# A hybrid decoder step on one core: two more weight slots, key turns and weights moved ahead of state traffic, first merge's products beside its gate

## The reference

```python
h = rms_norm(x, lw['norm_w'])
proj = jnp.einsum('bsd,de->bse', h, lw['w_in']) + lw['b_in']
# A: gated DeltaNet (conv, chunks of the delta rule, per-head state), gate dn_z
# B: RG-LRU (conv, gates, scan), gate lru_g
# C: forgetting attention: fq = rms_norm(fq), fk = rms_norm(fk), fv, decay logf, gate fg
# M: cross-attention into 256 memory tokens, gate mg
mk, mv = jnp.split(jnp.einsum('bmd,de->bme', rms_norm(mem, w), w_mem_kv), 2)   # prompt's memory keys, values
branches = jnp.stack([out_a, out_b, out_c, out_m], axis=2)
up = jnp.einsum('bsnw,nwd->bsnd', branches, lw['w_branch'])
gates = jax.nn.sigmoid(mgate.reshape(bn, s, N_BRANCH, D_MODEL))
y = x + jnp.einsum('bsd,de->bse', jnp.sum(gates * up, axis=2), lw['w_out'])
```

## Time and profile before

| | us |
|---|---|
| median of 3 runs (1779.48 to 1781.74) | 1780.54 |
| the profiled execution | 1779.63 |
| its span, first to last instruction | 1777.9 |
| PE busy in it (95%) | 1683.3 |
| PE loading weights (90%, beside the matmuls) | 1609.0 |
| DVE busy (44%) | 787.0 |
| ACT busy (30%) | 533.3 |
| POOL busy (29%) | 512.5 |

### The profile page before, as it was taken

One profiled execution on the slowest core, in us unless ns is written; L12 is line 12 of the kernel. 1 busy time (PEld: TensorE's weight loads), 2 busy tenths in 40 slices (PEclk: granted clock), 3 DMA queues, 4 the chain that ended last, 5 costly groups with the idle time before them and its releaser, 6 DMA issues. The chain is left out here.

```text
span 1777.9 us, 26816 instructions
## 1 busy us (share of the span) xinstructions
PE 1683.3 (95%) x11027; PEld 1609.0 (90%) x11027; DVE 787.0 (44%) x1199; ACT 533.3 (30%) x895; POOL 512.5 (29%) x388
## 2 busy tenths in 40 slices
PE   5999998999999998899999999999999989999999
PEld 5899998999999998899889898999989988899976
DVE  5485742333333334550365511145657540744711
ACT  6223333222222222132234323221145212554300
POOL 1343325333344314511344431212211121012310
PEclk9999999999999999899999999999999999999999
DMA  4211144222222115423255341234310332433531
GB/s 135 49 39 48 48 131 134 66 66 66 54 66 66 48 48 160 142 72 92 88 165 154 104 146 66 90 96 154 84 47 14 108 96 66 142 98 114 159 94 54
DMA packets 189367, 163.21 MB, mean 92 GB/s; under 512 B 18381, under 2 KB 157056, under 8 KB 188727
## 3 DMA queue, kind: packets, MB, share of 16 engines
q1 hardware_dynamic: 189246, 161.51, 31.0%
HBM read 131.38 MB, written 30.22 MB: 91 GB/s over the span
## 5 line engine op out<-in xcount | busy, mean ns | idle before, releaser
L258 POOL TENSOR_TENSOR wL<-w_raw,wH 128x1024 fp32r<-128x1024 f32 (+1 forms) x114 | 247.4, 2170 | 887.6 <-ACT wH L251 887.6
L282 PE MATMUL ps<-hH,wH 128*128 128x344 f32 x1920 | 449.3, 343 | 27.0 <-POOL wL L258 11.0
L282 PE MATMUL ps<-hL,wH 128*128 128x344 f32 x1920 | 412.2, 323 | 0.0
L282 PE MATMUL ps<-hH,wL 128*128 128x344 f32 x1920 | 409.8, 322 | 0.0
L282 PEld LDWEIGHTS ps<-hH,wH 128*128 128x128 f32 x1920 | 315.1, 192 | 40.5 <-issue 23.6
L282 PEld LDWEIGHTS ps<-hL,wH 128*128 128x128 f32 x1920 | 328.3, 191 | 0.0
L282 PEld LDWEIGHTS ps<-hH,wL 128*128 128x128 f32 x1920 | 325.3, 190 | 0.0
L251 ACT ACTIVATE wH<-w_raw 128x1024 fp32r<-128x1024 f32 (+1 forms) x120 | 112.7, 939 | 124.4 <-PE ps L282 99.3
L2743 POOL TENSOR_SCALAR fa_logits<-fox_c_bc,token_scalars 128x128 f32<-128x128 f32 (+7 forms) x32 | 58.2, 1820 | 67.5 <-PE ps L2768 50.1
L2886 DVE SCALAR_TENSOR_TENSOR fa_logits<-ps,fox_rq,fa_logits 128x512 f32<-128x512 f32 (+3 forms) x48 | 28.2, 612 | 106.5 <-POOL fa_logits L2744 59.6
L1730 ACT ACTIVATE d_m<-ps 128x512 f32<-128x512 f32 x48 | 28.6, 595 | 142.3 <-PE ps L1906 142.3
(11 more groups left out here) (558 smaller groups left out, 2815.2 us busy)
## 6 DMA issues: line engine op xcount, KB each, us to landing
w_raw<-in_w_in SPq DMA_DIRECT2D x80, 512.0 KB, 5.3
m_th<-gate_spill SPq DMA_DIRECT2D x28, 516.0 KB, 4.3
gate_spill<-d_gate SPq DMA_DIRECT2D x18, 516.0 KB, 3.0
fa_kv<-in_cache_fox_k SPq DMA_DIRECT2D x32, 256.0 KB, 3.1
fa_kv<-in_cache_fox_v SPq DMA_DIRECT2D x32, 256.0 KB, 3.1
w_raw<-in_w_branch SPq DMA_DIRECT2D x32, 256.0 KB, 2.9
gate_spill<-fa_gate SPq DMA_DIRECT2D x10, 516.0 KB
x_rows<-in_x_prompt SPq DMA_DIRECT2D x8, 512.0 KB, 6.5
```

Of the source, the lines that this page charges most:

```text
L258: pool.tensor_tensor(self.wL[:, t % 2, 0:nk], self.raw[:, t % 2, 0:nk], self.wH[:, t % 2, 0:nk].bitcast(F32), ALU.subtract).then_inc(self. ...
L282: last = pe.matmul(self.ps[:, b + g, 0:cols], w[:, t % 2, k], x[:, k, g * cols:(g + 1) * cols], start=(k == 0 and n == 0), stop=(k == nk - ...
```

## The change

Four edits that do not touch what is computed.

1. *Memory tiles.* Tiles 2, 3, 6 and 7 of the 8 memory tiles get raw slots of their own (2 and 3) in y_x, the memory rows' buffer, which is free when the 8 transposes are done (`raw_free`, mem_tr). wH and wL keep two slots. SP asks for the first two memory tiles ahead of the first two stores of the dn_z gate, and for tiles 2 and 3 ahead of the third. POOL no longer makes the low part of memory tile 1; DVE now makes those of tiles 1 to 7 (before: 2 to 7).
2. *fk.* The load of the fourth fk tile stands between the two halves of the decode state loads, and that of the first fv tile ahead of the wait for the query row. `POOL_AT` puts one state before the low part of fk tile 2 instead of three, three before that of fk tile 3 instead of six, and six before that of fv tile 0 instead of eight.
3. *fv.* ACT copies out the first five turns before it calls `before(act)`, which now stands ahead of the first tile's own copy.
4. *fg and the first merge.* DVE multiplies gate and branch right behind each gate part, and ACT rounds three of the four products inside the fg stage.

The tiles d_state, d_dT and d_w of the delta rule lie elsewhere in the on-chip buffer, so that they don't overlap y_x.

```diff
     def loads(self, sp, upto):
...
-            if t >= 2:
-                sp.wait_ge(self.w_lo, t - 1)
-            sp.dma_start(self.raw[:, t % 2, 0:nk], src).then_inc(self.w_loaded[t % 2], 16)
+            q, n, last = self.raw_use(t)
+            if t in self.raw_free:
+                sp.wait_ge(*self.raw_free[t])
+            if last is not None:
+                sp.wait_ge(self.w_lo, last + 1)
+            sp.dma_start(self.raw_at(t)[:, 0:nk], src).then_inc(self.w_loaded[q], 16)
...
+    def raw_slot(self, t):
+        return self.raw_of[t][0] if t in self.raw_of else t % 2
+
+    def raw_at(self, t):
+        return self.raw_of[t][1] if t in self.raw_of else self.raw[:, t % 2]
+
+    def raw_use(self, t):
+
+        q = self.raw_slot(t)
+        users = [u for u in range(t) if self.raw_slot(u) == q]
+        return q, len(users), users[-1] if users else None
...
@@ gate_branch
+                K.loads(sp, t0 + 4 + 2)
                 if spill is not None:
                     put(0)
                     put(1)
                 if side:
                     side.sync_last(sp)
-                K.loads(sp, t0 + 4 + 2)
                 if spill is not None:
+                    K.loads(sp, t0 + 4 + 4)
                     put(2)
-                    K.loads(sp, t0 + 4 + 3)
+                    K.loads(sp, t0 + 4 + 5)
                     put(3)
...
-                K.split_lo(pool, t0 + 4 + (2 if next_by_dve else 1))
+                K.split_lo(pool, t0 + 4 + 1)
...
                     act.activation(TH[:], G[:, slot(j)], ACT.Tanh).then_inc(th, 1)
+                    if then and j >= 1:
+                        then.act_hi(act, j - 1)
...
                     dve.scalar_tensor_tensor(g, TH[:], 1.0, g, ALU.add, ALU.mult).then_inc(silu, 1)
+                    if then:
+                        dve.wait_ge(silu, j + 1)
+                        then.dve_product(dve, j)
...
@@ Merge
-            for j in range(H):
+            for j in range(H - 1 if self.begun else 0, H):
                 self.br.act_hi(act, j)
...
-            if j < H:
+            if j < H and not self.begun:
                 self.br.dve_product(dve, j)
...
@@ UnitsAndMemory
+        for x, q in ((2, 2), (3, 3), (6, 2), (7, 3)):
+            K.raw_of[t_kv + x] = (q, self.X[:, q - 2].rearrange("p (k c) -> p k c", k=KD))
+            if x < 4:
+                K.raw_free[t_kv + x] = (self.Y["tr"], KD)
...
@@ DeltaDecode
-    POOL_AT = ((0, 1, 2), (3, 4, 5), (6, 7), ())
+    POOL_AT = ((0,), (1, 2), (3, 4, 5), (6, 7))
...
@@ project_tiles
-                    side.sync_first(sp)
+                    side.sync_first(sp, 0)
+                    K.loads(sp, t0 + 4)
+                    side.sync_first(sp, 1)
                     for j in range(2):
-                        K.loads(sp, t0 + 4 + j)
+                        K.loads(sp, t0 + 5 + j)
                         side.sync_part(sp, j)
...
-                    if j == 0 and fresh is None:
+                    if j == 0 and turned_first:
+                        act.wait_ge(*ready)
+                    elif j == 0 and fresh is None:
                         before(act)
...
                     for turn in of(j):
                         turns.act(act, turn)
+                    if j == 0 and turned_first:
+                        before(act)
                     act.wait_ge(K.tile_done, t + 1)
```

More of the change, by code:

```diff
@@ L152, in __init__ @@
         self.dn_convs = self.dn_space.enter_context(nc.sbuf_tensor("dn_conv_states", [P, 12, 24], F32))
-        self.w_loaded = [sem("w_loaded0"), sem("w_loaded1")]
+        self.w_loaded = [sem(f"w_loaded{q}") for q in range(4)]
         self.w_hi, self.w_lo = sem("w_hi"), sem("w_lo")
@@ L159, in __init__ @@
         self.at_load = self.at_hi = self.at_lo = 0
+        self.raw_of, self.raw_free = {}, {}
         self.v_sem, self.v_n = sem("vector_step"), [0]
@@ L247, in split_hi @@
             nk = self.tiles[t][1]
-            act.wait_ge(self.w_loaded[t % 2], 16 * (t // 2 + 1))
+            q, n, _ = self.raw_use(t)
+            act.wait_ge(self.w_loaded[q], 16 * (n + 1))
             if t >= 2:
                 act.wait_ge(self.tile_done, t - 1)
-            act.activation(self.wH[:, t % 2, 0:nk], self.raw[:, t % 2, 0:nk], ACT.Identity).then_inc(self.w_hi, 1)
+            act.activation(self.wH[:, t % 2, 0:nk], self.raw_at(t)[:, 0:nk], ACT.Identity).then_inc(self.w_hi, 1)
             self.at_hi = t + 1
@@ L905, in gate_branch @@
 def gate_branch(K, t0, name, G, tag, side=None, spill=None, fetch=None, fresh=False,
-                next_by_dve=False):
+                next_by_dve=False, then=None):
     nc = K.nc
@@ L1041, in __init__ @@
     def __init__(self, K, sb, t0, n, br, here, first=False, prepared=False, nxt=None, fetch=None,
-                 late=None):
-        self.late = late
+                 late=None, begun=False):
+        self.late, self.begun = late, begun
         self.K, self.t0, self.n, self.br, self.here = K, t0, n, br, here
@@ L1477, with __init__ @@
 class UnitsAndMemory(UnitFactors):
-    def __init__(self, K, kept, c, tail):
+    def __init__(self, K, kept, c, tail, t_kv):
         super().__init__(K, kept, c)
@@ L1572, in delta_rule @@
         two = lambda n_: sb(n_, [P, 2, H, P])
-        X, Y, ST, DT, W, M1, U, STG, O, SQ = (one(n_) for n_ in (
-            "_x", "_y", "_state", "_dT", "_w", "_m1", "_u", "_st_decayed", "_o", "_osq"))
+        X, Y, M1, U, STG, O, SQ = (one(n_) for n_ in ("_x", "_y", "_m1", "_u", "_st_decayed", "_o", "_osq"))
         NU, QKT, QG, VB, KBG, KD_ = (two(n_) for n_ in ("_nu", "_qkT", "_qgT", "_vb", "_kbg", "_kdec"))
+        ST, DT, W = (one(n_) for n_ in ("_state", "_dT", "_w"))
         RN, GC = units.RN, units.GC
@@ L2050, in load_rows, with sync_first @@
                      src.broadcast_to([P, n * H * P])).then_inc(sem, 16)
-    def sync_first(self, sp):
-        for b in range(NB):
+    def sync_first(self, sp, half):
+        for b in range(NB // 2 * half, NB // 2 * (half + 1)):
             if b % (NB // 2) == 0:
@@ L2343, in project_tiles @@
                   preload=True, side=None, late=None, ready=None, first=None, settle=None,
-                  fresh=None, early=(), by_dve=False):
+                  fresh=None, early=(), by_dve=False, turned_first=False):
     nc = K.nc
@@ L3176, in build @@
                 project_tiles(K, at["fv"], 4, BROW["fv"], VX, "fv", turns=turns,
-                              rows=(k_rows, sizes, K.knw, after), late=decode, ready=K.emptied(at["fv"] - 1),
+                              rows=(k_rows, sizes, K.knw, after), late=decode, ready=K.emptied(at["fv"] - 1), turned_first=True,
                               stores=[((turns.normed, j + 1), d, k_rows[j])
@@ L3201, in build @@
                 with K.gate_buffer("c_gate") as G:
-                    gate_branch(K, at["fg"], "fg", G[0], "gc", fetch=(GA[0], K.d_z, z_in))
+                    in_c = BranchIn(K, "m2", G, K.merged, None)
+                    gate_branch(K, at["fg"], "fg", G[0], "gc", fetch=(GA[0], K.d_z, z_in), then=in_c)
                     with nc.sbuf_tensor("c_low", [P, H, TOK], F32R) as LO:
-                        merge_branch(K, at["merge2"], 2, BranchIn(K, "m2", G, K.merged, LO), here[2], first=True,
-                                     nxt=in_a)
+                        in_c.L = LO
+                        merge_branch(K, at["merge2"], 2, in_c, here[2], first=True, nxt=in_a, begun=True)
                 merge_branch(K, at["merge0"], 0, in_a, here[0], prepared=True)
```

4 lines of the change are left out of this document (2 added, 2 removed).

## The result

The changed kernel takes 1763.05 us (median of 4 runs, 1761.34 to 1764.75). The kernel before, run beside it, takes 1780.01 (1778.54 to 1781.74). The ratio is 0.9909, 95% interval [0.9894, 0.9924]: 16.2 us faster, where 15.1 were forecast. The execution profiled after is the slowest of its four: 1764.75 us, span 1763.1, clock 0.986 (before 1779.63, 1777.9, 0.983).

A forecast was written before the change was run, and what follows sets the result against it. TensorE bounds the kernel (busy 1683.3 us), so only its pauses and low clock can be won. Gains 3.3 + 8.0 + 3.8 = 15.1 from 1779.63 give 1764.5, plus 0.9 for the median: 1765.4 us, range 1759 to 1773.

The forecast's parts named there:

- 3.3 forecast: Memory tiles: 27.4 us instead of 30.7 up to the first gate tile, a gain of 3.3 (bounds 0 and 5).
- the 1.5 of low clock behind the first pause: Memory tiles: 1.5 us lost at the 1.2 GHz level after the pause behind tile 0, taken as before the change.
- The 0.9 allowed for meetings with POOL: Memory tiles: 0.9 us for DVE's low parts slowed beside POOL's delta rule preparation; bounds 0 and 3.9.
- The rival on which the gain is eaten: Memory tiles: DVE's low parts that meet POOL's preparation eat the gain; 1768.7 us in all, chance 0.14.
- forecast 8.8 us earlier: fk: both pauses and their low clock go for a new pause of 0.5; fv tile 0 starts at 727.3, not 736.13.
- 8.0: fk and fv together: the third row is normed at 768.3 instead of 776.26, a gain of 8.0 us.
- its upper bound (DVE undisturbed by POOL): fk and fv together: a gain of 9.6 us if POOL does not disturb DVE.
- The rival of a late vector chain: fv: last states or query row come later, so DVE's chain starts four microseconds later; 1769.4 us in all, chance 0.11.
- The stalls only move: fk's gain is given back in fv, memory tiles gain nothing, only the merge gains; 1777 us in all, chance 0.05.
- Weights that land at 765: fv tile 2: weights landing after 765 instead of 746 make the kernel over 0.2% slower; chance 0.07.
- 3.8 forecast: First merge: TensorE's pause of 2.3 and 1.5 of low clock go, a gain of 3.8 us; lower bound 2.3.

The follow-up runs named there:

- e3_mem: The changed kernel with all parts undone but the memory tiles' (raw slots, load places, DVE's second low part); ratio 0.9972 to the kernel before.
- f3_squares: The changed kernel with more early turn copies on ACT in fv, and VectorE making sums of key rows 0 to 4 early; ratio 0.9898 to the kernel before.
- e1_fk: The changed kernel with all undone but fk's part (POOL's order of states, weight load); ratio 1.0000 to the kernel before.
- f1_no_fk: The changed kernel with only fk's part undone; ratio 0.9908 to the kernel before.

## Why the prediction was right

**Memory tiles**, 3.3 forecast, 4.9 in the first pair of profiles, 4.5 over all. The mechanism held step by step: first pause 2.67 (2.65), none for weights, one of 1.03 ahead of the gate tile (1.3). The mis-sized term is the 1.5 of low clock behind the first pause. In three of ten profiles a stretch at the low clock followed it and the stage took 26.7 to 26.8; in the other seven 25.7 to 25.9. The 0.9 allowed for meetings with POOL was near: the short pauses at tiles, 0.50 and 0.88, are 1.4. In the three profiles with the low clock TensorE is busy for 22.0 to 22.3 us (22.5 forecast) and the short pauses make 0.7 to 0.9, so there the terms hold nearly as they stand. The rival on which the gain is eaten is out by e3_mem. Its mechanism exists, though: two DVE rows of f3_squares end 0.5 us behind POOL's low parts, after 2.58 and 2.81 us in place of 0.7. The Trainium skill (SBUF — State Buffer, section "SBUF: two separate sides") states it as a lock: of a DVE instruction with two inputs on the chip and a GpSimd instruction, the one that starts second waits for the whole of the other. These rows agree with it.

**fk.** Both pauses went as worked out, and the new one is 0.76 (0.5). The start of fv tile 0, forecast 8.8 us earlier, came 9.0 earlier by the clock of the kernel before. That this is worth nothing alone and at most 1.5 us beside fv's part is in the prediction only by way of its sum, in which the later chain decides. e1_fk and f1_no_fk show it.

**fv.** Against the clock of the kernel before, 5.4 us ahead at the gate tile, the state wait ended at 744.5 (744.2 forecast), TensorE resumed at 749.2 (748.4) after 4.98 us (4.6), the sums were done at 759.6 (759.2), and the third turn back began at 769.3 (768.3). So 7.0 instead of the **8.0**: a microsecond in the norms' start and length. In part this is luck. The forecast took the length of the squares and of the norms from the kernel before, where one square (759.60, 2.44 us) and the third row's norm had met a low part on POOL:

```profile
772.50 2.88 DVE L2482 TENSOR_TENSOR merged<-merged,fv_rn 128x512 f32<-128x512 f32 x1
...
772.30 2.53 POOL L258 TENSOR_TENSOR wL<-w_raw,wH 128x1024 fp32r<-128x1024 f32 x1 [10.81 <-ACT wH L251]
```

So 2.2 of the 6.4 us up to the third norm were such a meeting, which the prediction counts in only by way of its upper bound (DVE undisturbed by POOL). After the change there was again one in the squares (2.12) and one in the norms (2.87), the latter on the second row, so that TensorE's last wait is for that row. The waits for L2484, now L2517, are two as forecast. The rival of a late vector chain is this same chain with four more microseconds, of which one came. "The stalls only move" holds for fk alone; fv's part gave its 7. Weights that land at 765 didn't occur: 742.2 by the profile after.

**First merge**, 3.8 forecast: the wait is gone, the clock 1.00, and the profiles with and without it differ by 4.3 in the rest of the span and by 3.8 from this merge on, each of them with some 2 us of chance.

**Sum.** 15.1 forecast; by the terms as measured 4.5 + 7.0 + 4.3 = 15.8, by the ratio 16.2, between the two profiled executions 14.9. The sum is nearer than its terms: the memory tiles gave 1.2 more and fv 1.0 less than forecast.

## What to carry to other kernels

Ahead of a bound, a pause removed is a lead, not a gain: look for the next thing that the engine must wait for in absolute time, and test the parts both alone and left out of the whole. When that bound is a chain on VectorE, look at which of its rows are longer than their like, at what runs on GpSimd at that moment, and move that work to a place where the chain has slack. With a clock that varies between executions, compare a stretch between two fixed points of TensorE's work, not the whole span, and trust a difference of a microsecond or two only where single rows show it.

## What was not expected of the hardware

The same pause at the same place is followed by the 1.2 GHz level in one profile and not in another: behind the 2.67 us pause in the memory tiles in three of ten (the kernels are alike up to there), behind the pause of 1.75 in the kernels without that part in all four. The profiles of the changed kernel, with the same pauses, have granted clocks of 0.986 and 0.990, and the unchanged rest of their spans differs by 2.6 us.

A VectorE instruction of 8 partitions, 0.68 us in the changed kernel, took 2.58 us beside a low part on GpSimd, as much as rows of 128 partitions did (2.0 to 2.9): its length there was set by POOL's instruction, not by its own size. Not every VectorE row is held: the sum at 743.44 in the changed kernel (L2511), which has one input where the squares and norms have two, lies wholly beside the low part of 743.37 and takes its usual 0.69 us.
